# Three 1024 x 1024 products of a two-block transformer kernel, computed by seven products of quarters instead of eight

## The reference

```python
# end of the first block
ple_gate = sigmoid(rmsnorm(x, ln_ple) @ w_ple_gate)
x = x + (p @ w_ple_proj) * ple_gate
# second block, values of the tokens
v = (h @ w_in)[:, V columns]          # then split in 16 heads
# end of the second block
y = merged @ w_o
x = x + gt * rmsnorm(y, post_g)
```

## Time and profile before

| | us |
|---|---|
| median of 3 runs (lowest, highest) | 1256.1 (1255.47, 1256.13) |
| the profiled execution's own time | 1256.2 |
| its span, first to last instruction | 1254.3 |
| TensorE busy in the span | 1192.9 |
| VectorE busy | 310.6 |
| ScalarE busy | 212.4 |
| GpSimd busy | 109.7 |

### The profile page before, as it was taken

The page is one execution under the profiler, slowest core; times in us unless marked ns, Lnnn a source line. Parts: engine busy times, 40 slices in busy tenths (PEclk is TensorE's granted clock), DMA queues, the critical chain, the costliest instruction groups (busy, mean ns, idle before and its releaser), DMA issues.

```text
span 1254.3 us, 14608 instructions
## 1 busy us (share of the span) xinstructions
PE 1192.9 (95%) x6020; PEld 825.1 (66%) x6020; DVE 310.6 (25%) x670; ACT 212.4 (17%) x436; POOL 109.7 (9%) x118
## 2 busy tenths in 40 slices
PE   6999999999999999998988889899999999999998
PEld 6887888887345454433333323688888888876687
DVE  2136357414010101110201010220001016536612
ACT  2232653112000000000100000220000000035501
POOL 0025234001000000000000000000000000125300
PEclk9999999999999999998999999999999999999999
DMA  9999333293899999999999999844444444544300
GB/s 323 331 289 316 101 101 102 101 392 108 349 407 408 413 409 417 415 419 415 421 415 420 416 419 397 264 138 165 142 160 148 155 157 146 178 132 126 102 1 34
DMA packets 149718, 324.59 MB, mean 259 GB/s; under 512 B 8736, under 2 KB 111264, under 8 KB 133280
## 3 DMA queue, kind: packets, MB, share of 16 engines
q1 hardware_dynamic: 143920, 316.32, 67.4%
q0 software_dynamic: 1536, 4.20, 1.2%
q10 hardware_dynamic: 4208, 3.31, 0.8%
HBM read 322.75 MB, written 1.05 MB: 258 GB/s over the span
## 4 chain that ended last, share of the span: by engine, by line
PE 87%; DMA 7%; ACT 2%; issue 2%; DVE 1%; POOL 0%; SPq 0%; DVEq 0%; POOLq 0%; ACTq 0%
PE bank L582 34%; PE bank L869 16%; PE bank L585 13%; PE bank L908 8%; DMA AR<-in_w 6%; PE bank L848 3%; PE bank L881 2%; PE bank L946 1%; PE bank L1005 1%; PE bank L992 1%; PE bank L884 1%; PE bank L1025 1%; PE bank L1038 1%; PE bank L648 1%; ACT AR L1257 1%
## 5 line engine op out<-in xcount | busy, mean ns | idle before, releaser
L582 PE MATMUL bank<-HT,ring 128*128 128x256 f32 x1760 | 383.9, 379 | 0.0
L582 PEld LDWEIGHTS bank<-HT,ring 128*128 128x128 f32 x1760 | 333.1, 190 | 44.7 <-issue 0.4
L869 PE MATMUL bank<-ring,AR 128*64 128x512 f32 x640 | 177.6, 611 | 18.1 <-DMA AR<-in_w 13.2
L869 PEld LDWEIGHTS bank<-ring,AR 128*64 128x64 f32 x640 | 56.1, 140 | 123.0 <-issue 122.4
L869 PE MATMUL bank<-AR 128*64 128x512 f32 x384 | 119.4, 613 | 0.1
L585 PE MATMUL bank<-ring,AR 128*128 128x256 f32 (+1 forms) x392 | 88.1, 387 | 11.5 <-DMA ring<-in_w_in 9.5
L908 PE MATMUL bank<-ring,AR 128*64 128x512 f32 x384 | 87.7, 599 | 11.3 <-ACT AR L1257 11.3
L585 PEld LDWEIGHTS bank<-ring,AR 128*128 128x128 f32 x392 | 75.4, 198 | 22.3 <-DMA ring<-in_w_in 9.5
L1865 DVE TENSOR_TENSOR AR<-AR,bank 128x256 f32<-128x256 f32 x32 | 13.5, 421 | 285.3 <-ACT AR L1248 284.5
L1394 POOL TENSOR_TENSOR SM<-SM 128x2 f32<-128x2 f32 (+3 forms) x8 | 11.6, 1448 | 699.2 <-DVE SM L1512 658.9
L585 PE MATMUL bank<-ring,HT 128*128 128x256 f32 x320 | 70.5, 380 | 0.0
(11 more groups left out here) (324 smaller groups left out, 1008.3 us busy)
## 6 DMA issues: line engine op xcount, KB each, us to landing
ring<-in_w SPq DMA_DIRECT2D x128, 1024.0 KB, 16.4
AR<-in_w SPq DMA_DIRECT2D x64, 1024.0 KB, 17.2
ring<-in_w_in SPq DMA_DIRECT2D x62, 1024.0 KB, 5.2
ring<-in_w_mod SPq DMA_DIRECT2D x12, 1024.0 KB, 9.1
AR<-in_w_in SPq DMA_DIRECT2D x5, 1024.0 KB, 17.1
ring<-in_w_out SPq DMA_DIRECT2D x4, 1024.0 KB, 5.2
ring<-in_w_ple_gate SPq DMA_DIRECT2D x4, 1024.0 KB, 9.5
ring<-in_w_out_conv SPq DMA_DIRECT2D x4, 1024.0 KB, 5.3
```

Of the source, the lines that this page charges most:

```text
L582: mm = pe.matmul(bank[:, part * T:part * T + T], w[:, k, c0 + part * P:c0 + part * P + P], act[:, k, :], start=(k == 0), stop=(k == k_n - 1))
L869: mm = pe.matmul(bank[e * SLOT:e * SLOT + SLOT, :].rearrange("p (w n) -> p w n", w=2), XG[:, k, :], w, start=(k == 0), stop=(k == DK - 1))
```

## The change

Write the product as quarters, C = A W with A in four (two halves of the tokens by two halves of the depth) and W in four (two halves of the depth by two halves of the columns). A piece is now one quarter of the weight, 512 deep and 512 wide, again 1 MB, and they come in the order W11, W22, W12, W21. TensorE makes seven products of quarters, each of 4 matmuls of 512 columns:

- P1 = A11 W11, P2 = A12 W21
- P3 = S4 W22, P5 = S1 T1, P6 = S2 T2, P7 = S3 T3, P4 = A22 T4, in this order

The sums of the activations (`operand_sums`) are S1 = A21 + A22, S2 = S1 - A11, S3 = A11 - A21, S4 = A12 - S2, each over 128 x 512. The sums of the weights are T1 = W12 - W11, T3 = W22 - W12, T2 = W22 - T1, T4 = W21 - T2, each over 128 x 2048, written in place over W11, W12, W22 and W21 in the ring. ScalarE copies P1 out (`first_copy`), and VectorE makes the results' quarters: C11 = P1 + P2, U2 = P1 + P6, U = U2 + P5, C12 = U + P3, C22 = U + P7, U3 = U2 + P7, C21 = U3 + P4. What read the results in PSUM reads these quarters in SBUF. The core of it:

```diff
+        def quarters(w, name):
+            for i, j in ((0, 0), (1, 1), (0, 1), (1, 0)):
+                fill((w[:, 4 * i:4 * i + 4, 512 * j:512 * j + 512], 4, 512), name=name, feature=False, ncols=512)
...
+        SEVEN = ["ple", "v2", "wo"]
+        SEVEN_BANKS = {"ple": B[0:4], "v2": B[4:8], "wo": B[4:8]}
...
+        STEPS = ["S", "T1", "C11", "T2", "C12", "C22", "U3", "C21"]
+        QUARTERS = ((0, 0, "C11"), (0, 1, "C12"), (1, 1, "C22"), (1, 0, "C21"))
...
+                if f - RING in summed_until:
+                    sp.wait_ge(S("seven_dve"), summed_until[f - RING])
```

TensorE (`part` is the 4 matmuls over the depth, 512 columns each):

```diff
+            def seven(name, act, sums, ahead=None, first=None):
...
+                wait_slot(pe, f11)
+                part(bank[0], quarter(0, 0, ahead), f11).then_inc(S("seven_ps"), 1)
+                wait_slot(pe, f21)
+                part(bank[1], quarter(0, 1, ahead), f21).then_inc(S("seven_ps"), 1)
+                wait_slot(pe, f22)
+                pe.wait_ge(S("seven_dve"), step(name, "S"))
+                part(bank[2], summed(3), f22).then_inc(S("seven_ps"), 1)
+                pe.wait_ge(S("seven_dve"), step(name, "T1"))
+                part(bank[3], summed(0), f11).then_inc(S(ready_sem(p5)[0]), 1)
+                pe.wait_ge(S("seven_dve"), step(name, "T2"))
+                part(bank[0], summed(1), f22).then_inc(S(ready_sem(p6)[0]), 1)
+                part(bank[1], summed(2), f12).then_inc(S(ready_sem(p7)[0]), 1)
+                pe.wait_ge(S("seven_dve"), step(name, "C12"))
+                part(bank[2], quarter(1, 1), f21).then_inc(S(ready_sem(p4)[0]), 1)
...
-            for i in of["ple"]:
-                product(i, PLT, first=True, ahead=two_engines("pleT_dve", "pleT_act") if i == of["ple"][0] else None)
+            seven("ple", PLT, PLS, ahead=two_engines("pleT_dve", "pleT_act"))
...
-            turn_rows(cols(HN))
+            turn_rows(cols(HN), halfway=lambda: wait_emptied(of["vc"][-1]))
...
-            products("v2", HT)
+            seven("v2", HT, V2S)
             pe.wait_ge(S("roped"), 8)
-            for i in of["v2"]:
-                pe.wait_ge(S("emptied_" + emptied[i][0]), emptied[i][1])
+            pe.wait_ge(S("seven_dve"), step("v2", "C21"))
```

VectorE:

```diff
+            def seven(name, after=lambda n: None, parts=1):
...
+                wait_slot(dve, f12)
+                dve.wait_ge(S("seven_ps"), ps + 1)
+                V_.tensor_tensor(w11, w12, w11, ALU.subtract).then_inc(S("seven_dve"), 1)
+                wait_slot(dve, f22)
+                V_.tensor_tensor(w12, w22, w12, ALU.subtract)
+                dve.wait_ge(S("seven_ps"), ps + 2)
+                dve.wait_ge(S("seven_act"), SEVEN.index(name) + 1)
+                V_.tensor_tensor(c11, c21, bank[1][:, :], ALU.add).then_inc(S("seven_dve"), 1)
+                dve.wait_ge(S("seven_ps"), ps + 3)
+                dve.wait_ge(S("seven_dve"), step(name, "C11"))
+                V_.tensor_tensor(w22, w22, w11, ALU.subtract).then_inc(S("seven_dve"), 1)
+                dve.wait_ge(S("seven_dve"), step(name, "T2"))
+                wait_slot(dve, f21)
+                V_.tensor_tensor(w21, w21, w22, ALU.subtract)
+                after(0)
+                wait_result(dve, p6)
+                link(V_.tensor_tensor(c21, c21, bank[0][:, :], ALU.add))
+                link(V_.tensor_tensor(UT, c21, bank[3][:, :], ALU.add))
+                V_.tensor_tensor(c12, UT, bank[2][:, :], ALU.add).then_inc(S("seven_dve"), 1)
+                wait_result(dve, p7)
+                V_.tensor_tensor(c22, UT, bank[1][:, :], ALU.add).then_inc(S("seven_dve"), 1)
+                V_.tensor_tensor(c21, c21, bank[1][:, :], ALU.add).then_inc(S("seven_dve"), 1)
+                after(1)
+                after(2)
+                wait_result(dve, p4)
+                dve.wait_ge(S("seven_dve"), step(name, "U3"))
+                for part in range(parts):
+                    c = slice(512 // parts * part, 512 // parts * (part + 1))
+                    V_.tensor_tensor(c21[:, c], c21[:, c], bank[2][:, c], ALU.add).then_inc(S("seven_dve"), 1)
+                after(3)
```

`operand_sums` runs for `ple` behind the turned rows of `PLT`, for `v2` behind those of `HT` (long before the product), and for `wo` when `GA` is complete. `after(n)` is, in `ple`, the multiplication and the sum into `X` of quarter n. In `wo` it is this, with C21 made and squared in two parts:

```diff
+            def out_after(n):
+                if n == 1:
+                    out_gain(0)
+                    out_norm(0)
+                    out_gain(1)
+                    for half in range(2):
+                        out_final(0, half)
+                if n == 2:
+                    out_gain(2)
+                if n == 3:
+                    out_gain(3, 0, 2)
+                    out_norm(1)
+                    out_gain(3, 1, 2)
+                    for half in range(2):
+                        out_final(1, half)
```

More of the change, by code:

```diff
@@ L333, in build @@
         NRA = len(results)
-        for c in range(4):
-            fill(wcols(a["w_ple_gate"], 256 * c, 256), name="ple", feature=False)
+        quarters(a["w_ple_gate"][0].rearrange("(k p) n -> p k n", p=P), "ple")
         for c in (2, 3):
@@ L346, in build @@
             fill(wcols(a["w_out_attn_2"], 256 * c, 256), name="yattn")
-        for c in range(4):
-            fill(wcols(a["w_o_2"], 256 * c, 256), name="wo", feature=False)
+        quarters(a["w_o_2"][0].rearrange("(k p) n -> p k n", p=P), "wo")
         NC_ = len(fills) - NA
@@ L593, in products, with part, quarter, column @@
                     product(i, act, ahead=ahead if i == of[name][0] else None)
+            def seven(name, act, sums, ahead=None, first=None):
+                p5, p6, p7, p4 = of[name]
+                n = SEVEN.index(name)
+                def part(bank, stationary, f):
+                    for k in range(4):
+                        mm = pe.matmul(bank[:, :], stationary(k), slot_view(f)[:, k, :], start=(k == 0), stop=(k == 3))
+                    return mm
+                def quarter(t, j, ahead=None):
+                    def column(k):
+                        if ahead is not None:
+                            ahead(4 * j + k)
+                        return act[:, 4 * j + k, t * P:t * P + P]
+                    return column
+                def summed(m):
+                    return lambda k: sums[:, m, k, :]
+                f11, f22, f12, f21 = [results[i][1] for i in of[name]]
+                bank = SEVEN_BANKS[name]
+                if n:
+                    pe.wait_ge(S("seven_dve"), step(SEVEN[n - 1], "C21"))
+                wait_slot(pe, f11)
[12 more added lines that the diff above has]
+                part(bank[2], quarter(1, 1), f21).then_inc(S(ready_sem(p4)[0]), 1)
             def pairs_of(sem, base=0):
@@ L1028, in _ @@
             products("yattn", HT, ahead=lambda k: pe.wait_ge(S("na_o"), k + 1))
[L1029 to L1040, removed]
+            seven("wo", GA, WOS, ahead=pairs_of("merged2"))
         @block.scalar
@@ L1361, in _ @@
                 turned_weights(n)
[L1362 to L1366, removed]
+            first_copy("wo")
+            for n, (t, half, what) in enumerate(QUARTERS):
+                parts = 2 if n == 3 else 1
+                for part in range(parts):
+                    act.wait_ge(S("seven_dve"), step("wo", what) + part)
+                    c = slice(512 * half + 256 * part, 512 * half + 256 * part + 512 // parts)
+                    nc.scalar.activation(HN[:, t, c], YF[:, t, c], ACT.Square, accum_out=SSY[:, t, half + 2 * part:half + 2 * part + 1])\
+                      .then_inc(S("y_sq"), 1)
         M_TMP_K = area(M0, 4, TT, MH * 16)
@@ L2029, in out_final @@
                                         op0=ALU.mult, op1=ALU.add).then_inc(S("final"), 1)
[L2032 to L2038, removed]
+            def out_after(n):
[13 more added lines that the diff above has]
+                        out_final(1, half)
+            dve.wait_ge(S("merged2"), 4)
+            operand_sums(GA, WOS)
+            seven("wo", after=out_after, parts=2)
 _NAMES = ["x", "p", "positions", "ln_mix", "w_in", "hg_lb", "hg_onorm", "w_oA", "mla_qa_norm", "mla_kva_norm", "w_uq",
```

118 lines of the change are left out of this document (81 added, 37 removed).

## The result

1248.05 us (median of 6 runs, 1246.78 to 1251.11) against 1255.84 (median of 6 runs, 1254.24 to 1256.13): ratio 0.9942 with a 95% interval of 0.9929 to 0.9954, 7.3 us (5.8 to 8.9) faster by the ratio and 7.8 by the medians. The profiled execution took 1248.66 us, its span is 1246.8.

What follows compares the result with a forecast made beforehand. TensorE's matmuls were taken to bound all three changed stretches. Savings of 3.5 us (`ple`), 3.4 (`v2`) and 1.2 (`wo`) sum to 8.1, so 1256.1 becomes 1248.0 us, range 1246.6 to 1250.5.

Steps and rivals of the forecast that it cites:

- The pace: TensorE in each product: 56 records at 430.6 ns take 24.11 us, saving 3.52 us if TensorE never waits.
- The long sums: VectorE's 2048-element sums of the weights in the ring take 2.29 us each, all hidden under the matmuls.
- The bound of 3.9: Upper bound in us for one long sum, if everything ran as the sum of 1024 beside GpSimd.
- the second rival: Slower, chance 0.05: long sums of 4.6 us make TensorE wait 4.3 us per product and the clock fall; 1266 us.
- The slack: Time VectorE's sums have to spare before TensorE wants them: 0.9 us ahead of P6, 1.1 us ahead of P4.
- GpSimd in `v2`: Three GpSimd additions of 0.72 us beside T1 and T3 could lengthen these by 2.2 us at most; slack covers it.
- The chain behind `ple`: VectorE's steps from `ple`'s results to the normalized rows end later but stay hidden behind `vc`, with 6 us left.
- The end: Behind `wo`, VectorE's late work leaves 1.2 us of the 3.5 saved, between 0.6 and 1.7.
- The clock at the start of `ple`: `ple` takes 1.76 us more than its sisters, with the clock at 1.2 GHz after a TensorE pause; left unchanged.
- the first two: The second rival, and before it: same time, chance 0.09, long sums of 3.9 us, TensorE waits 2.2 us per product, 1254.6.
- The third: Faster by less, 0.08 together with the fourth: covers at the ends fail, 1251.5 us behind `ple` or 1249.2 in `wo`.
- The fourth: Change not as stated, 0.08 together with the third: records at 437 ns save 0.4 us less per product, 1249.1 us.

Runs made afterwards that it cites:

- experiment 7: Changed kernel with six GpSimd additions of 128 x 1024 from the start of `v2`: 1260.24 us in one execution, `v2` 36.68 us.
- experiment 5: Changed kernel with one more VectorE pass over W22 ahead of T2 in `v2`: 1251.87 us in one execution, `v2` 26.61 us.
- experiment 4: Changed kernel with the four long sums of the weights left out or cut to two columns: ratio 0.9944 to the kernel before.
- experiment 6: Changed kernel with three more VectorE passes over W22 ahead of T2 in `v2`: 1258.24 us in one execution, `v2` 34.06 us.
- the two profiles without the pause: Turned rows written ahead of the mean: in the changed kernel with VectorE's end reordered too, 1244.54 us; in the kernel before, 1252.99 us.

## Why the prediction was right

Forecast 1248.0 us, measured 1248.05. That the two agree to 0.1 us is luck: 8.1 us were worked out, 7.9 stand in the three stretches and 7.5 in the spans, the forecast started from a median of 1256.1 where the six runs give 1255.84, and the gain itself is known only to 5.8 to 8.9 us. What was right is the mechanism, TensorE's saving with VectorE's sums under it, and the terms one by one:

- **The pace.** 430.6 ns per record were taken from the experts' matmuls, 429.2 were measured. What follows `ple` and `v2` starts 3.58 and 3.50 us sooner, where 3.5 and 3.4 were worked out.
- **The long sums.** 2.29 us by extending the line through 512 and 1024 elements; 2.28 to 2.29 measured in eleven of twelve. The bound of 3.9 was not needed here, and it was no bound: beside a busy GpSimd (experiment 7) two long sums took 4.42 and 4.46, near the 4.6 of the second rival.
- **The slack.** 0.9 us ahead of P6 and 1.1 ahead of P4 were worked out; in `v2` the trace has 0.93 (1096.33 to 1097.26) and 1.09 (C12's end at 1103.04, P4's first matmul at 1104.13). Experiment 5 used it up, at 0.77.
- **GpSimd in `v2`.** Up to 2.2 us were allowed for T1 and T3. Only T3 was hit, with 2.81 us (and a sum of the rope ahead of T1, with 1.22 in place of 0.69). T1 ran for 1.2 us beside GpSimd's additions and kept its 2.29. GpSimd gave way more: its two additions beside T1 and T3 took 4.51 us together and not 1.44. The slack covered it, as argued.

```profile
1085.75 1.22 DVE L2089 TENSOR_TENSOR AR<-AR,CST 128x512 f32<-128x512 f32 x1
1087.60 2.29 DVE L1624 TENSOR_TENSOR ring<-ring 128x2048 f32<-128x2048 f32 x1
1088.69 4.51 POOL L1558 TENSOR_TENSOR AR<-AR,CST 128x256 f32<-128x256 f32 x2 [2.28 <-DMA AR<-in_bias]
1089.81 2.81 DVE L1626 TENSOR_TENSOR ring<-ring 128x2048 f32<-128x2048 f32 x1
```

- **The chain behind `ple`.** 6 us of cover were worked out. The normalized rows are ready at 826.19 (824.77 + 1.42), and TensorE takes them at 833.11, 6.9 us later.
- **The end.** 1.2 us were worked out for `wo`, 0.83 came, inside the stated 0.6 to 1.7. This is the mis-sized term: the last two final sums were to start 28.22 us behind the first matmul of `wo` and start at 28.59. The rows of the changed kernel:

```profile
1235.17 0.69 DVE L1642 TENSOR_TENSOR AR<-AR,bank 128x512 f32<-128x512 f32 x1 [1.30 <-PE bank L645]
...
1237.22 0.68 DVE L2149 TENSOR_TENSOR AR<-AR,PG 128x512 f32<-128x512 f32 x1
1237.39 0.95 POOL L1564 TENSOR_TENSOR SM<-SM 128x1 f32<-128x1 f32 x1 [64.12 <-DVE SM L2154]
1238.44 1.41 DVE L2161 SCALAR_TENSOR_TENSOR HN<-AR,SM,X 128x512 f32<-128x512 f32 x2 [0.53 <-POOL SM L1564]
1239.77 0.69 DVE L2149 TENSOR_TENSOR AR<-AR,PG 128x512 f32<-128x512 f32 x1
1240.37 0.75 DVE L1650 TENSOR_TENSOR AR<-AR,bank 128x256 f32<-128x256 f32 x2
...
1242.18 0.67 POOL L1564 TENSOR_TENSOR SM<-SM 128x1 f32<-128x1 f32 x1 [3.85 <-DVE SM L2154]
1242.96 1.42 DVE L2161 SCALAR_TENSOR_TENSOR HN<-AR,SM,X 128x512 f32<-128x512 f32 x2 [0.52 <-POOL SM L1564]
```

  P4's last matmul ends at 1238.57, but C21 waits until 1240.37 for the work of the first 128 tokens, the 1.7 us (1.8 here) that the prediction named. Of the 0.37 us, 0.23 are there by C21 (26.00 us behind the first matmul, 25.77 worked out). What it missed is the power: 0.95 and 0.67 us, where I had taken the 0.56 of the earlier trace rows. VectorE waits for both, 0.53 and 0.52 us. The first now runs beside a gain with two SBUF inputs (1237.22), the second beside the half gain. In all nine profiles with `wo` by seven products the two take 0.95 and 0.67 us, and in the four with the old end, where the gain beside them reads a bank, 0.56 or 0.57. That the gain's SBUF inputs are the cause is argued from this and from experiment 7, not tried by itself.
- **The clock at the start of `ple`.** I left its 1.76 us in both kernels, since nothing ahead was changed. It fell in both profiles, so this came out even, but not for my reason: see below.

Of the rivals, the first two are refuted for this kernel by the rows (long sums of 2.29 us, no wait ahead of P6 or P4) and by experiments 4 and 5. They stay true as conditions: experiments 6 and 7 made the waits, and the clock was low behind each. The third came true in the part that the forecast had already counted, `wo`. The fourth asked for 437 ns per record, and 429.2 were measured. One step of the second rival was worked out wrong: a long sum of 4.1 us as the point where the gain turns leaves out the clock, which the rival itself counts. With its 1.8 us per product the turn is at a wait of (8.1 - 5.4) / 3 = 0.9 us, a long sum of 3.5 us.

## What to carry to other kernels

Where TensorE is busy for a whole stretch and VectorE works a fifth of it, one product in eight can be traded for sums (this scheme is Winograd's form of Strassen's product), if each long sum is drawn against the matmul that wants it; here 28.0 us of long sums, 49 us of VectorE's time in all (310.6 to 359.6), bought 7.3 us, with 0.9 us of slack at the narrowest place. In this kernel the trade paid in the middle of a chain of products and hardly at its end, because the last results come late and together: look there at the engine behind the matmuls, and put its instructions in the order in which others wait. And before such sums are put beside GpSimd's work, add up GpSimd's time: in experiment 7 the sums out of SBUF ahead of T2 each waited 2.1 to 2.5 us for it, nearly as much again as a long sum's own 2.29.

## What the runs showed that I had not expected

- **The clock behind one and the same pause falls only sometimes.** TensorE stands still for 1.8 us ahead of `ple` in nine of the eleven kernels run here and in the two kernels themselves. In those eleven profiles the granted clock fell in five (25.97 or 29.55 us for `ple`) and stayed at 1.00 in six (24.27 or 27.86), in changed and unchanged kernels alike: 1.7 us between two executions of one kernel. The two groups are parted by when `ple` began: between 792.96 and 793.49 us in the five, between 793.83 and 795.99 in the six. No run here tries why. In the two profiles without the pause it stayed, and two are too few to prove that the pause makes the difference. A pause of 1.3 us (experiment 5) had no fall; behind those of 2.1, 4.3 and 5.9 us the clock was low. The Trainium skill warns of long gaps between bursts of matmuls ("TensorE: Matmul & The Clock Gate", section "Why this matters for your kernels"); the traces agree, and show that a short one can be enough.
- **GpSimd and VectorE hold each other up, by about one instruction at a time**: beside GpSimd's additions of 1024, VectorE's sum of 512 took 2.75 to 3.21 us in place of 0.69, its sum of 2048 4.4 in place of 2.29, and GpSimd's addition 3.24 (19.45 / 6), where the kernel before has one of 1.94. So many short sums suffer more than a few long ones. A sum with one operand in PSUM took 0.68 beside it.
- **TensorE's pace did not change under VectorE's sums** in the same slots of the ring: 429.2 ns per record with them, and without them (experiment 4) the same stretches within 0.01 us, where the clock was the same.
